# Stick-breaking attention: the sum over later key blocks moves from TensorE to VectorE

## The reference

```python
z = jnp.einsum('bhqd,bhkd->bhqk', q_blk, k_pre) * (HEAD_DIM ** -0.5)
causal = s_idx < t_idx
log_1m_beta = jnp.where(causal, jax.nn.log_sigmoid(-z), 0.0)
tail = lax.cumsum(log_1m_beta, axis=3, reverse=True) - log_1m_beta
a = jnp.where(causal, jnp.exp(jax.nn.log_sigmoid(z) + tail), 0.0)
return jnp.einsum('bhqk,bhkd->bhqd', a, v_pre)
```

## Time and profile before

| | us |
|---|---|
| median of 3 runs | 1079.54 (1079.44 to 1079.77) |
| the profiled execution | 1079.7 |
| its span, from the first to the last instruction | 1078.0 |
| TensorE busy | 1065.1 |
| VectorE busy | 618.7 |
| ScalarE busy | 510.1 |
| the mixer's heads, first L1721 to the end of the last | 420.0 to 602.7 |

### The profile page before, as it was taken

The page is one execution under the profiler, slowest core; times in us unless marked ns, Lnnn a source line. Parts: engine busy times, 40 slices in busy tenths (PEclk is TensorE's granted clock), DMA queues, the critical chain, the costliest instruction groups (busy, mean ns, idle before and its releaser), DMA issues.

```text
span 1078.0 us, 15248 instructions
## 1 busy us (share of the span) xinstructions
PE 1065.1 (99%) x4982; PEld 891.5 (83%) x4982; DVE 618.7 (57%) x1043; ACT 510.1 (47%) x930; POOL 9.2 (1%) x29
## 2 busy tenths in 40 slices
PE   9999999999999999999999999999999999999997
PEld 7888888888888878888888888888888888888886
DVE  5454445444222689696969889554455445333655
ACT  6333333333222558686869746433333334333645
POOL 1000000000020000000000000000000000000000
PEclk9999999999999999999999999999999999999999
DMA  6333333332222332232312122333332333444002
GB/s 213 92 88 107 97 97 88 103 97 97 95 97 97 79 88 71 77 79 67 84 53 63 54 81 82 105 96 99 97 97 82 112 117 131 155 135 146 1 20 79
DMA packets 100948, 100.24 MB, mean 93 GB/s; under 512 B 7696, under 2 KB 83216, under 8 KB 100912
## 3 DMA queue, kind: packets, MB, share of 16 engines
q1 hardware_dynamic: 100912, 99.77, 30.7%
HBM read 94.44 MB, written 2.10 MB: 90 GB/s over the span
## 4 chain that ended last, share of the span: by engine, by line
PE 89%; DVE 5%; ACT 3%; issue 2%; DMA 0%; DVEq 0%; SPq 0%; ACTq 0%
PE bank L1419 28%; PE bank L1421 27%; PE bank L1420 27%; PE bank L1721 2%; PE bank L1736 1%; DVE w_r L925 1%; DVE scratch L1317 1%; PE bank L1635 1%; PE bank L1688 0%; DVE big L1097 0%; PE bank L1754 0%; DVE big L1094 0%; DVE acc L945 0%; PE bank L1690 0%; DVE scratch L1088 0%
## 5 line engine op out<-in xcount | busy, mean ns | idle before, releaser
L925 DVE TENSOR_TENSOR w_r<-w_raw,w_r 128x512 fp32r<-128x512 f32 x332 | 225.1, 690 | 381.5 <-ACT w_r L508 381.3
L508 ACT ACTIVATE w_r<-w_raw 128x512 fp32r<-128x512 f32 x332 | 204.4, 628 | 406.2 <-PE bank L1421 401.8
L1419 PE MATMUL bank<-xg,w_r 128*128 128x512 f32 x890 | 349.4, 393 | 0.3 <-DVE scratch L1088 0.3
L1420 PE MATMUL bank<-xg,w_r 128*128 128x512 f32 x890 | 346.8, 390 | 0.0
L1421 PE MATMUL bank<-xg,w_r 128*128 128x512 f32 x890 | 346.8, 390 | 0.0
L1419 PEld LDWEIGHTS bank<-xg,w_r 128*128 128x128 f32 x890 | 167.1, 188 | 36.1 <-issue 1.4
L1421 PEld LDWEIGHTS bank<-xg,w_r 128*128 128x128 f32 x890 | 167.1, 188 | 35.1
L1420 PEld LDWEIGHTS bank<-xg,w_r 128*128 128x128 f32 x890 | 167.2, 188 | 34.4 <-issue 0.7
L1419 PE MATMUL bank<-big,w_r 128*128 (+2 forms) x420 | 163.8, 390 | 0.1
L1421 PE MATMUL bank<-big,w_r 128*128 (+2 forms) x420 | 162.8, 388 | 0.0
L1420 PE MATMUL bank<-big,w_r 128*128 (+2 forms) x420 | 162.8, 388 | 0.0
(11 more groups left out here) (169 smaller groups left out, 963.6 us busy)
## 6 DMA issues: line engine op xcount, KB each, us to landing
w_raw<-in_ffn_w_gate SPq DMA_DIRECT2D x88, 256.0 KB, 2.8
w_raw<-in_ffn_w_up SPq DMA_DIRECT2D x88, 256.0 KB, 2.8
w_raw<-in_ffn_w_down SPq DMA_DIRECT2D x88, 256.0 KB, 2.6
w_raw<-in_w_in SPq DMA_DIRECT2D x36, 256.0 KB, 3.0
scratch<-in_w_ple_gate SPq DMA_DIRECT2D x16, 256.0 KB, 3.2
w_raw<-in_w_in SPq DMA_DIRECT2D x24, 128.0 KB, 2.2
big<-big SPq DMA_DIRECT2D x24, 128.0 KB, 2.2
w_raw<-in_w_out SPq DMA_DIRECT2D x8, 256.0 KB, 2.6
```

What stands on the lines that cost most here:

```text
L508: act.activation(w_slot(0, slot, 0, 4 * P), w_raw[:, slot, :], ACT.Copy).then_inc(w_hi, 1)
L925: dve.tensor_tensor(w_slot(1, slot, 0, 4 * P), w_raw[:, slot, :], plain(w_slot(0, slot, 0, 4 * P)), SUB).then_inc(w_lo, 1)
L1419: pe.matmul(dst, w_hi_ap, m_hi, start=start, stop=False, skip_group_check=True)
L1420: pe.matmul(dst, w_lo_ap, m_hi, start=False, stop=False, skip_group_check=True)
```

## The change

For query column t the sums of the later blocks are the same for each row of a key block: key block c needs the softplus of all blocks after it. VectorE now adds these up first. After the change the softplus of block 3 is added to that of block 2 (the last 128 columns of it), and the result to that of block 1 (its last 256 columns), in place in `spf`. The sums are rounded like all else: ScalarE makes the high parts, VectorE the remainders, into `later_r`, a free part of the output tiles. TensorE then has four triangular pairs of matmuls, and one full pair for each of blocks 2, 1 and 0: for block 2 with the softplus of block 3 as it is, for blocks 1 and 0 with the sums. That is 14 matmuls for 20.

The rounding goes in the order of banks 1, 2, 0, so that blocks 1 to 3 have been rounded before they are overwritten; the two additions stand on VectorE between the remainder of bank 2 and that of bank 0. Blocks 1 and 3 change places within bank 1, so that what is added lies in one piece.

```diff
-Z_AT = {0: (0, 0, 512), 1: (1, 0, 384), 3: (1, 384, 128), 2: (2, 0, 256)}
-Z_BANKS = [[0], [1, 3], [2]]
+Z_AT = {0: (0, 0, 512), 3: (1, 0, 128), 1: (1, 128, 384), 2: (2, 0, 256)}
+Z_BANKS = [[0], [3, 1], [2]]
+ROUND_ORDER = [1, 2, 0]
...
+        later_r = [[oT[i][:, TILES - 1, 0:3 * P], oT[i][:, 2 * TILES - 1, 0:2 * P]] for i in range(2)]
+        later_sum = [spf[:, 512 + P:1024], spf[:, 1024:Z_COLS]]
...
-                for b in range(3):
+                for b in ROUND_ORDER:
                     c = slice(512 * b, 512 * b + Z_W[b])
                     act.wait_ge(sp_full, 3 * hd + b + 1)
                     act.activation(sp_r[0][:, c], spf[:, c], ACT.Copy).then_inc(sp_hi, 1)
+                for i, c in enumerate((1, 0)):
+                    act.wait_ge(sum_done, 2 * hd + i + 1)
+                    act.activation(later_r[0][c], later_sum[c], ACT.Copy).then_inc(sum_hi, 1)
...
             def softplus_lo(hd):
-                for b in range(3):
+                for i, b in enumerate(ROUND_ORDER):
+                    if i == 2:
+                        third, second = slice(512, 512 + P), 512 + P
+                        last = 1024
+                        dve.wait_ge(sp_lo, 3 * hd + 2)
+                        dve.tensor_tensor(spf[:, last + P:last + 2 * P], spf[:, last + P:last + 2 * P], spf[:, third],
+                                          ADD).then_inc(sum_done, 1)
+                        dve.wait_ge(sum_done, 2 * hd + 1)
+                        dve.tensor_tensor(spf[:, second + P:last], spf[:, second + P:last], spf[:, last:last + 2 * P],
+                                          ADD).then_inc(sum_done, 1)
                     c = slice(512 * b, 512 * b + Z_W[b])
-                    dve.wait_ge(sp_hi, 3 * hd + b + 1)
+                    dve.wait_ge(sp_hi, 3 * hd + i + 1)
                     dve.tensor_tensor(sp_r[1][:, c], spf[:, c], plain(sp_r[0][:, c]), SUB).then_inc(sp_lo, 1)
+                for i, c in enumerate((1, 0)):
+                    dve.wait_ge(sum_hi, 2 * hd + i + 1)
+                    dve.tensor_tensor(later_r[1][c], later_sum[c], plain(later_r[0][c]), SUB).then_inc(sum_lo, 1)
...
                     for c in range(TB):
                         b, at, w = Z_AT[c]
-                        for jc in range(c, TB):
-                            jb, jat, jw = Z_AT[jc]
-                            off = at + (jc - c) * P
-                            lhs = tri_r if jc == c else full_r
-                            for part in range(2):
-                                last = pe.matmul(Z[b][:, off:off + jw], lhs, sp_r[part][:, 512 * jb + jat:512 * jb + jat + jw],
-                                                 start=False, stop=(jc == TB - 1 and part == 1), skip_group_check=True)
+                        for part in range(2):
+                            pe.matmul(Z[b][:, at:at + w], tri_r, sp_r[part][:, 512 * b + at:512 * b + at + w],
+                                      start=False, stop=False, skip_group_check=True)
+                    for part in range(2):
+                        pe.matmul(Z[2][:, P:2 * P], full_r, sp_r[part][:, 512:512 + P],
+                                  start=False, stop=False, skip_group_check=True)
+                    for i, dst in enumerate((Z[1][:, 2 * P:512], Z[0][:, P:512])):
+                        pe.wait_ge(sum_lo, 2 * hd + i + 1)
+                        for part in range(2):
+                            last = pe.matmul(dst, full_r, later_r[part][1 - i], start=False, stop=part == 1, skip_group_check=True)
                     last.then_inc(tri_done, 1)
```

More of the change, by code:

```diff
@@ L248, in build @@
             "z_done", "absz", "exp_z", "lnz", "sp_full", "sp_hi", "sp_lo", "tri_done", "a_exp", "a_hi", "a_lo"))
+        sum_done, sum_hi, sum_lo = map(sem, ("sum_done", "sum_hi", "sum_lo"))
         l_done, neg_max, p_exp, rcp, p_scaled, pt_done, pt_hi, pt_lo = map(sem, (
```

## The result

The changed kernel takes 1086.85 us (median of 4 runs, 1084.21 to 1087.17) against 1079.65 for the kernel before (4 runs, 1079.44 to 1080.09). The ratio is 1.0059, with a 95% interval of 1.0048 to 1.0071: slower by 0.6%. The profiled execution took 1086.8 us, its span is 1085.1 against 1078.0.

What follows compares the result with a forecast made beforehand. TensorE bounds the kernel, busy 1065.1 of 1078.0 us. Head 0 +1.6, heads 1, 3, 5 -1.8, heads 2, 4 +1.3, head 6 +0.9, head 7 +1.6 sum to +3.6: 1083.2 us, range 1079.0 to 1086.8.

Steps and rivals of the forecast that it cites:

- spared for 0.6: TensorE's sums, every head: six fewer matmuls save 0.6 us, bounds 0.43 to 0.68.
- the 1.6 in heads 0 and 7: logits(1) in heads 0 and 7: VectorE has no gap, so its extra 1.58 us lands on TensorE, +1.6 each.
- 0.66: logits(1) in heads 2 and 4: first maximum 1.41 us later against a margin of 0.79, +0.66 each.
- 0.93 in head 6: weigh in head 6: VectorE's remainders 1.42 us later, margin 0.54, hand-over 0.05; stated as +0.9.
- the 0.1 us gap behind the remainders: VectorE's queue behind L1114: 0.1 us gaps close up, so the delay is 1.41 us instead of 1.58.
- The prices for the 128 and 384 columns: VectorE's added instructions: 0.29 us for 128 columns (bounds 0.28 to 0.42), 0.55 us for 384.
- a rival with a chance of 0.25: Clock: TensorE's new waits bring half clock, most likely at heads 0 and 7; 1084.8 to 1086.4 us, chance 0.25.
- both its steps: Half clock at head 0 and at head 7: +1.6 us for one, +3.2 for both.
- ScalarE's copies: Two added copies of 256 and 384 columns, some 0.9 us beside VectorE's remainders: cost nothing; uncovered, up to 0.5 before L768.
- The list of what would show it: Expected trace signs: sums group 2.1 to 2.2 us in odd heads, exponential waits some 6 us, VectorE's odd-head gap about 0.4.
- five times VectorE's extra time: Whole sum: about five times VectorE's extra time per head less 4.3 us, zero at 0.86 us extra.

Runs made afterwards that it cites:

- the kernel with the shorter queue: Changed kernel with VectorE's second output remainder and sum of squares, tiles 0 to 2, moved behind the fourth softmax row: 1082.19 us.
- 11, 5 and 7 filling products: Changed kernel plus unused 128-column products in the last tile: 11 before head 6's sums, 5 behind them, 7 behind head 7's sums; 1084.24 us.
- both kernels made from it by a move: Kernel before with logits(1) between the projection's halves and the fourth maximum later, 1081.42 us; kernel before with VectorE's second output remainder and sum of squares later, 1080.16 us.

## Why the prediction was right, and where it was off

**The sign and its cause.** The forecast was slower, 1083.2, because the work that the change gives VectorE stands ahead of the maxima in a queue without a pause. The two halves by themselves show it: the added work alone costs 6.5 us, the spared matmuls alone give 3.5. And with 1.3 us of other work taken out of that queue, the wait is gone in heads 2 and 4.

**The size.** The forecast said +3.6 us, the medians say +7.2 and the ratio 6.4. The median of 1086.85 lies 0.05 us beyond the stated range, which ended at 1086.8; by the ratio it is 1085.9. The single number, 1083.2, was about half of the step. The steps of the sum held: 0.63 us spared for 0.6, 1.6 for the 1.6 in heads 0 and 7, 0.79 and 0.80 for 0.66, 1.04 for 0.93 in head 6 at a whole clock. Heads 2 and 4 came out 0.14 too low since I let the 0.1 us gap behind the remainders close; L1257 starts 0.09 behind L1133 again, and the delay is 1.59 and not 1.41. The prices for the 128 and 384 columns, 0.29 and 0.55, are those of the trace after; the Trainium skill (VectorE: DVE Perf Modes, the section on the TRN2 errata) has (N + 151)/0.96 ns for an fp32 tensor_tensor, by which they are an estimated 0.29 and 0.56, and the rows agree.

**The term that was left out** is the clock. I put it into a rival with a chance of 0.25 and left it out of the forecast. With both its steps that rival gave 1086.4. The measured time is the rival's sum: 1.31 us in head 6 and 1.44 to 1.6 in head 7 (1.57 against the kernel with the shorter queue, whose clock stayed whole behind nearly the same wait). That it came to nearly the rival's number is in part luck. Its places were half right. I had named heads 0 and 7. In the profiled execution after it was head 7, and in head 6 the half clock that had cost 0.52 us, since VectorE's results were due shortly behind the sums that it lay on, moved on to a projection that nothing else held up. In head 0, with waits of 1.65 and 1.64 us close together, it came in the profiled execution of one kernel (with 11, 5 and 7 filling products; 1.6 us, logits(1) to weigh took 7.54 us for 5.93) and not in the changed kernel's own. One run of the changed kernel at 1084.21 beside three at 1086.8 to 1087.2 fits a run with one or both stretches less; no trace of it was taken, so this is not shown.

**ScalarE's copies** were put at nothing, since they end before VectorE's remainders, with 0.5 us ahead of L768 at most. They put L768 back by 1.58 us in head 2 (1.35 us behind the first softplus copy before, 2.93 after) as well as in head 6. In the heads with a pause of ScalarE this costs nothing, as forecast; in head 6 it is one of the two queues behind the wait of 1.34 us, and the one that stays when VectorE's is cleared.

**What a signal said.** The list of what would show it held for the most part: the group at 2.13 us; the new line of waits, 7.5 us over heads 0, 2, 4, 6 and 7, for the 6 that I had put in heads 0, 2, 4 and 7 (head 6, which I had bound at weigh instead, waits 1.34 us there, for ScalarE's queue as much as for VectorE's); L1721's wait in head 0 doubled to 1.65 and in head 6 to 2.89; VectorE's pause before L1095 in odd heads at 0.37, with 0.4 forecast; nothing on `sum_lo`. The rule of thumb in the forecast, that five times VectorE's extra time arrives, was too simple: the instruction added to test it came through with its 0.34 us in two heads and with 0.14 in three.

## What to carry over

An engine that is busy for 57% of the span can be the one on the path: look at the stretch between its last pause and the result that the bound engine waits for, and count what each added instruction pushes back there. Work taken off the bound engine pays only where the engine that gets it has a pause before the next hand-over; where it has none, first move out of its queue what nobody needs soon, and leave out the heads in which that isn't possible. A second queue can stand behind the first, nearly as late, as ScalarE's did in head 6. A wait of one or two microseconds on TensorE has a second price, the half clock that may follow, and it belongs into the sum wherever several come close together.

## What the runs showed of the hardware

- TensorE was granted half its clock for 3.4 us at a time, and in three kernels for 6.8. Ahead of each such stretch stood waits, but their length alone did not decide it. Before the sums of head 6 a wait of 2.10 to 2.12 us was followed by half clock in five profiled executions (the kernel before, both kernels made from it by a move, the 14 matmuls alone, the change in heads 1 to 5) and by none in a sixth (the change in heads 1, 3 and 5). Behind the sums of head 7, waits of 1.92 and 2.23 us were followed by it and one of 1.90 was not. In head 0, two waits of 1.63 to 1.68 us were followed by it in one profiled execution and not in three others, nor were 1.64 and 2.00 in a fifth. What else decides it was not found. Where the waits were filled with matmuls of no use, the clock stayed at 1.00.
- The lost time depends on what the half clock lies on. Over the sums of head 6 before, the group took 4.36 us and not 2.76, but only 0.52 us came through at weigh, which needs VectorE's results from about that time. Over work that nothing else held up, 1.3 to 1.6 us of 3.4 were lost.
- An fp32 product of 128 x 128 by 128 columns is two matmuls of 0.11 us in the trace, while one with the rounded type is one of 0.11.
